# Sums of squares of k and q as two fp32r products, and the first modulation pieces in another shape, in a two-block transformer kernel

## What is computed

```
c_act = silu(c)
mod = c_act @ ada_w[layer] + ada_b[layer]                  # c is 1024 wide, ada_w[layer] 1024 x 6144
sh_m, sc_m, g_m, sh_f, sc_f, g_f = split(mod, 6)
h = rms_norm(x, pre_mix_g) * (1 + sc_m) + sh_m             # the input of the first product
...
k = rms_norm(k, k_norm_g)                                  # over the 64 elements of each head
q = rms_norm(q, q_norm_g)                                  # likewise
```

## Time and profile before

| | |
|---|---|
| median of 3 executions | 2051.48 us |
| the profiled execution | 2050.17 us, of which its span is 2048.5 us |
| TensorE matmuls busy | 1962.9 us, 96% of the span |
| TensorE weight loads busy | 1680.9 us, 82% |
| GpSimd busy | 999.8 us, 49% |
| VectorE busy | 793.4 us, 39% |
| ScalarE busy | 721.9 us, 35% |
| start of the first fp32r product | 52.92 us |
| stages k, v, q | about 768 to 913 us |

### The profile page before, as it was taken

The page is one execution under the profiler, slowest core; times in us unless marked ns, Lnnn a source line. Parts: engine busy times, 40 slices in busy tenths (PEclk is TensorE's granted clock), DMA queues, the critical chain, the costliest instruction groups (busy, mean ns, idle before and its releaser), DMA issues. The chain is left out here.

```text
span 2048.5 us, 28257 instructions
## 1 busy us (share of the span) xinstructions
PE 1962.9 (96%) x10884; PEld 1680.9 (82%) x10884; DVE 793.4 (39%) x1391; ACT 721.9 (35%) x1163; POOL 999.8 (49%) x541
## 2 busy tenths in 40 slices
PE   5999999999999989999998999999999999999998
PEld 5998887888888878877877888888876988767998
DVE  5666533444444045443634101110327760136212
ACT  2324325322221264344536222222524323345324
POOL 1634654466674434456643655554423443534652
PEclk9999999999999999999999999999999999999999
DMA  7655543465656313232112333333232334311132
GB/s 260 206 165 165 165 164 114 149 180 175 194 176 210 96 54 94 73 103 88 53 37 64 111 92 99 96 93 96 79 76 65 94 99 99 89 52 32 63 98 89
DMA packets 220325, 230.71 MB, mean 113 GB/s; under 512 B 15456, under 2 KB 185224, under 8 KB 219960
## 3 DMA queue, kind: packets, MB, share of 16 engines
q1 hardware_dynamic: 215392, 213.28, 34.6%
q10 hardware_dynamic: 4824, 15.88, 2.3%
HBM read 226.33 MB, written 2.79 MB: 112 GB/s over the span
## 5 line engine op out<-in xcount | busy, mean ns | idle before, releaser
L752 POOL TENSOR_TENSOR w_lo<-raw,w_hi 128x1024 fp32r<-128x1024 f32 (+1 forms) x296 | 731.1, 2484 | 575.6 <-ACT w_hi L745 575.6
L1424 PE MATMUL acc<-hh,w_hi 128*128 128x512 f32 (+1 forms) x1472 | 558.4, 379 | 17.3 <-DVE hl L2096 9.6
L1424 PE MATMUL acc<-hh,w_lo 128*128 128x512 f32 (+1 forms) x1472 | 549.4, 373 | 0.0
L1424 PE MATMUL acc<-hl,w_hi 128*128 128x512 f32 (+1 forms) x1472 | 549.3, 373 | 0.0
L745 ACT ACTIVATE w_hi<-raw 128x1024 fp32r<-128x1024 f32 (+1 forms) x296 | 308.2, 1051 | 394.9 <-DMA raw<-in_ffn_w_down 152.9
L1424 PEld LDWEIGHTS acc<-hh,w_hi 128*128 128x128 f32 x1472 | 280.7, 191 | 76.5 <-issue 18.6
L1424 PEld LDWEIGHTS acc<-hh,w_lo 128*128 128x128 f32 x1472 | 280.6, 191 | 48.6
L1424 PEld LDWEIGHTS acc<-hl,w_hi 128*128 128x128 f32 x1472 | 280.9, 191 | 47.8 <-issue 1.7
L1957 DVE SCALAR_TENSOR_TENSOR ada_wide<-ada_raw,c_act,ada_wide 128x1024 f32<-128x1024 f32 x84 | 167.2, 1991 | 85.2 <-DMA ada_raw<-in_ada_w 56.8
L1424 PE MATMUL acc<-w_hi,hh 128*128 128x256 f32 x672 | 194.0, 289 | 3.3 <-POOL hl L1305 3.3
L1424 PE MATMUL acc<-w_lo,hh 128*128 128x256 f32 x672 | 191.5, 285 | 0.0
(11 more groups left out here) (535 smaller groups left out, 2954.6 us busy)
## 6 DMA issues: line engine op xcount, KB each, us to landing
raw<-in_ffn_w_gu SPq DMA_DIRECT2D x176, 256.0 KB, 3.3
raw<-in_w_in SPq DMA_DIRECT2D x52, 512.0 KB, 3.6
ada_raw<-in_ada_w SPq DMA_DIRECT2D x50, 512.0 KB, 4.1
raw<-in_ffn_w_down SPq DMA_DIRECT2D x44, 512.0 KB, 3.7
raw<-in_a_w_in SPq DMA_DIRECT2D x32, 512.0 KB, 3.7
ada_raw<-in_ada_w ACTq DMA_DIRECT2D x30, 512.0 KB, 5.8
raw<-in_a_w_out SPq DMA_DIRECT2D x16, 512.0 KB, 3.7
ada_raw<-in_kv_ada_w SPq DMA_DIRECT2D x16, 512.0 KB, 5.0
```

What stands on the lines that cost most here:

```text
L752: eng.tensor_tensor(w_lo[:, s, part, :], raw[:, s, part, :], w_hi[:, s, part, :].bitcast(F32), ALU.subtract).then_inc(w_split, 1)
L1424: ins = pe.matmul(out, w, x, start=first and n == 0, stop=last and n == len(pairs) - 1, skip_group_check=check)
```

## The change

1. The squares of k and q are written twice by ScalarE, in fp32 (`sq`) and in fp32r (`sq_hi`); GpSimd subtracts them into `sq_lo` in the place of `sq`, in a new epilogue of its own (`low_squares`); TensorE sums them by two fp32r products with `head_ones_r`, and waits for GpSimd.
2. The first 2048 columns of `mod` are cut in eight other pieces of 1 MB: 512 columns by 512 rows of `ada_w`, in rows of 2 KB. Five go to VectorE, 4 instructions of 512 columns each. Three go to TensorE, now with `c_act` as the stationary operand (one column) and the weights moving, so that the result is a row of 512; ScalarE copies two such rows to SBUF and TensorE turns them into columns by products with a 1x1 one. The order of loads, sums and features around them is new, and the first square root's table is loaded ahead of `x`. The first two units of `mlp_v` are split by ScalarE between the copies of `x_first`.
3. The high parts of the first four chunks of `h2` are made ahead of the last copy of v.
4. Some semaphores are joined (`last_x` into `x_ready`, `last_sg` into `sg_ready`, `last_std` into `std_ready`), with no instruction moved.

The diff, cut to its core:

```diff
 # SP
-            next_step(0)
-            whole_step(ada_first[:, 0], 0, ada_first_in[0])
-            next_step(1)
+            dve_unit(0)
+            pe_unit(0)
+            dve_unit(1)
             sp.dma_start(x_tok[:], ...).then_inc(x_landed, 16)
-            for s in range(1, ADA_PE):
-                whole_step(ada_first[:, s], s, ada_first_in[s])
+            pe_unit(1)
             sp.wait_ge(x_landed, 16)
-            for s in range(2, ADA_SETUP - ADA_PE):
-                next_step(s)
-            load_group(sp, "mlp_v", 0, 0)
+            dve_unit(2)
+            pe_unit(2)
+            dve_unit(3)
+            load_unit(sp, S["mlp_v"], src_of["mlp_v"], 0, 0, 0)
+            dve_unit(4)
+            load_unit(sp, S["mlp_v"], src_of["mlp_v"], 0, 0, 1)
             load_group(sp, "mlp_v", 0, 1)
 # ScalarE
             act.wait_ge(c_ps, 1)
+            act.activation(head_ones_r[:], head_ones[:], ACT.Copy)
             act.activation(c_act[:], aux[:, 0, 0:DC], ACT.Silu).then_inc(c_ok, 1)
...
+            act.activation(warm[:], eps[:], ACT.Sqrt)
             act.wait_ge(x_landed, 16)
...
+            for wide, src in enumerate((ada_ps, bank(1))):
+                act.wait_ge(row_ps, wide + 1)
+                act.activation(ada_first[0:1, wide, 0, :], src[0:1, :], ACT.Copy).then_inc(row_sb, 1)
             for k in range(DC):
                 act.wait_ge(xt_ps, k + 1)
                 act.activation(x_first[:, k, :], XT_BANKS[k % len(XT_BANKS)], ACT.Copy).then_inc(kept_ready, 1)
-            split_hi(act, S["mlp_v"], 0, 0)
+                if k < 2:
+                    split_hi(act, S["mlp_v"], 0, 0, slice(k, k + 1))
...
                     for m in range(2):
-                        act.activation(sq[:, m, :], sums(j)[:, m, :], ACT.Square).then_inc(hsq_ready, 1)
+                        act.activation(sq[:, m, :], sums(j)[:, m, :], ACT.Square)
+                        act.activation(sq_hi[:, m, :], sums(j)[:, m, :], ACT.Square).then_inc(hsq_ready, 1)
...
                 if (i, j) == (1, 1):
                     log_sigmoid(gl_f[:, 1, :], 1)
+                    hi_chunks("h2", KU, hh, free=lambda k: S["q"].unit0 - 1 + RING)
                 tokens_epilogue(v_fox)(st, i, j)
...
-            hi_chunks("h2", DC, hh, free=lambda k: S["q"].unit0 - (k < KU) + RING)
+            hi_chunks("h2", DC - KU, hh, KU, free=lambda k: S["q"].unit0 + RING)
 # GpSimd
-            lead(pool, "k", split_lo, nothing, "v", unroll=True, started=True)
+            def low_squares(c0):
+                def epi(st, i, j):
+                    for m in range(2):
+                        pool.wait_ge(hsq_ready, c0 + 4 * i + 2 * j + m + 1)
+                        pool.tensor_tensor(sq_lo[:, m, :], sq[:, m, :], sq_hi[:, m, :].bitcast(F32), ALU.subtract).then_inc(hsq_split, 1)
+                return epi
+            lead(pool, "k", split_lo, low_squares(0), "v", unroll=True, started=True)
...
-            lead(pool, "q", split_lo, nothing, "gate", unroll=True)
+            lead(pool, "q", split_lo, low_squares(8), "gate", unroll=True)
 # TensorE
-                        pe.matmul(bank(0)[:, 2 * s + m:2 * s + m + 1], ada_first[:, s, k, m * P:(m + 1) * P], c_act[:, k:k + 1],
-                                  start=k == 0, stop=k == DC - 1)
+                    ins = pe.matmul(dst, c_act[:, KU * half + k:KU * half + k + 1], ada_unit_home(s)[:, k, :],
+                                    start=half == 0 and k == 0, stop=half == 1 and k == KU - 1)
...
-                    pe.wait_ge(hsq_ready, t + 1)
+                    pe.wait_ge(hsq_split, t + 1)
                     if t >= 2:
                         pe.wait_ge(hstd, t - 1)
-                    pe.matmul(aux[:, t % 2, :], head_ones[:], sq[:, t % 2, :], start=True, stop=True).then_inc(hs_ps, 1)
+                    products(aux[:, t % 2, :], ((head_ones_r[:], sq_hi[:, t % 2, :]), (head_ones_r[:], sq_lo[:, t % 2, :])), True, True).then_inc(hs_ps, 1)
 # VectorE
+            ada_unit(0)
+            ada_unit(1)
+            for n, (dst, r) in enumerate(((par_a, 112), (par_b, 104), (par_c, 74))):
+                dve.wait_ge(par_t, n + 1)
+                dve.tensor_copy(dst[:, 0:r], bank(1 + n)[:, 0:r]).then_inc(par_ok, 1)
+            inverse_deviation(0)
...
+            ada_unit(2)
+            ada_unit(3)
+            ada_unit(4)
             dve.wait_ge(ada_first_ps, 1)
```

More of the change, by code:

```diff
@@ L156, in build_program @@
         head_ones = place("head_ones", [P, P])
+        head_ones_r = place("head_ones_r", [P, P], F32R)
         par_a = place("par_a", [P, 112])
@@ L1607, in wide_beside, with row_columns, setup_sums @@
                 return before_chunk
-            def column_sums(dst, src):
-                for m in range(2):
-                    ins = pe.matmul(dst[:, m:m + 1], src[:, m * P:(m + 1) * P], ones[:, 0:1], start=True, stop=True)
+            def row_columns(wide):
+                pe.wait_ge(row_sb, wide + 1)
+                for m in range(4):
+                    pe.matmul(bank(0)[:, 4 * wide + m:4 * wide + m + 1], ada_first[0:1, wide, 0, m * P:(m + 1) * P], ones[0:1, 0:1],
+                              start=True, stop=True)
+            def setup_sums(wide, at):
+                pe.wait_ge(ada_setup_ready, at)
+                for m in range(4):
+                    ins = pe.matmul(bank(0)[:, 4 * wide + m:4 * wide + m + 1], ada_setup[:, wide - 1, m * P:(m + 1) * P], ones[:, 0:1],
+                                    start=True, stop=True)
                 return ins
@@ L1646, in _ @@
                 pe.transpose(bank(1 + n)[:, 0:r], rows[0:r, n, :], ident[0:r, 0:r]).then_inc(par_t, 1)
+            setup_sums(2, 1)
+            row_unit(1, ada_ps[0:1, :]).then_inc(row_ps, 1)
             pe.wait_ge(par_ok, 3)
+            row_unit(2, bank(1)[0:1, :])
+            pe.wait_ge(ada_setup_ready, 2)
+            pe.matmul(bank(1)[0:1, :], ones[:, 0:1], ada_setup[:, 0, :], start=False, stop=True).then_inc(row_ps, 1)
+            row_columns(0)
             first_to_features()
[L1649 to L1654 removed]
             WS_BANKS = [aux[:, 0, :], aux[:, 1, :], ms[:], ada_ps[:]]
@@ L1966, in wide_finish, with ada_unit @@
             def wide_finish(q):
-                dve.wait_ge(ada_sum, ADA_SETUP - ADA_PAIRS + q + 1)
+                dve.wait_ge(ada_sum, q + 1)
                 cols = slice(2 * ADA_SETUP + DC * q, 2 * ADA_SETUP + DC * (q + 1))
                 dve.tensor_tensor(mod[:, cols], ada_ps[:, 0:DC], par_a[:, cols], ALU.add).then_inc(ada_col, 1)
[L1972 to L1975, removed]
-                    else:
-                        if kk:
-                            dve.drain()
-                        ins = dve.scalar_tensor_tensor(total, w[:, kk, :], c_act[:, k0 + kk:k0 + kk + 1], total, ALU.mult, ALU.add)
-                return ins
-            def ada_finish(step, par, summed):
-                dve.wait_ge(ada_sum, summed)
-                dve.tensor_tensor(mod[:, ds(2 * step, 2)], ada_ps[:, 2 * par:2 * par + 2], par_a[:, ds(2 * step, 2)], ALU.add) \
-                    .then_inc(ada_col, 1)
+            def ada_unit(n):
+                wide, half = ADA_DVE[n]
+                total = ada_setup[:, wide - 1, :]
+                dve.wait_ge(ada_next_in[n], 16)
+                for kk in range(KU):
+                    k = KU * half + kk
+                    if kk == 0 and (half == 0 or wide == 1):
+                        dve.tensor_scalar(total, ada_next[:, 1 + n, kk, :], c_act[:, k:k + 1], None, ALU.mult)
+                    else:
+                        dve.scalar_tensor_tensor(total, ada_next[:, 1 + n, kk, :], c_act[:, k:k + 1], total, ALU.mult, ALU.add)
+                    ins = dve.drain()
+                if half:
+                    ins.then_inc(ada_setup_ready, 1)
             def inverse_deviation(n):
```

98 lines of the change are left out of this document (47 added, 51 removed).

## The result

| | before | changed |
|---|---|---|
| median, us | 2050.54 (4 runs, 2048.11 to 2052.91) | 2035.78 (4 runs, 2033.00 to 2038.01) |
| ratio, 95% interval | | 0.9928 (0.9912 to 0.9944) |
| profiled execution, time / span, us | 2050.17 / 2048.5 | 2038.01 / 2036.3 |

The change takes 14.8 us off, with an interval of 11.5 to 18.0 us. The forecast was 2033.0, range 2028 to 2041: it is 2.8 us too low and inside its range. The profiled execution is the slowest of its four; its span is 12.2 us shorter than before.

The account below looks back on a forecast made before the run. The prediction took TensorE, hardly ever idle, as the bound. Setup 8.5, squares 6.4 and v to q 3.6 sum to 18.5 us, from 2050.17 to 2031.7; with the median 1.3 higher, 2033.0 us, range 2028 to 2041.

Parts of the forecast that it names:

- Squares: k and q: four fp32r matmuls replace two fp32 ones, 0.80 us saved for each of eight pairs, 6.4 us.
- the cover on GpSimd: k and q: the added square work stays hidden, with 3.7 us left before TensorE wants the next weights.
- rivals 2 to 4: k and q: late split or fp32 squares, 2039.4 each, together 0.09; GpSimd locked out by reciprocals, 2057, 0.03.
- From v to q: Start of q: earlier high parts of h2 remove TensorE's waits, 3.6 us less; 2 if GpSimd is late once.
- Setup: Start of the kernel: first product at 44.4 us instead of 52.92, 8.5 us less.
- The landing of VectorE's last piece: Setup: VectorE's last piece of weights lands at 33.0 us, or at 35.0 with 3.0 us a piece.
- GpSimd's splits fall onto this piece: Setup: two GpSimd splits at 34 to 39 us slow VectorE's last two instructions, ending at 39, not 36.3.
- the product 2.73 us later: Setup: the first product follows the start of normed at 40.6 us by 2.73 us, so at 43.3.
- The middle value of 44.4: Setup: first product's start, taken between 43.3 us and 45.4 us, the latter with 3.0 us a piece.
- rival 1: Setup: TensorE stays at half pace, first product at 48.7, setup gives 4.2 us, total 2037.3; chance 0.12.
- the sign of being wrong: Setup: first product starting past 48 us, with the features of x as what VectorE waits for.
- my doubt of it: Setup: old column products at half pace, though never idle, speak against sustained busy time raising the clock to 2.4 GHz.

Follow-up runs that it names:

- e4: Changed kernel without GpSimd's 16 subtractions, TensorE multiplying sq_hi twice: 2038.77 us, ratio 0.9934.
- e2: Kernel before the change with only the high parts of the first four h2 chunks made ahead of v's last copy: 2050.24 us, ratio 0.9993.
- e11: Held kernel without the early high parts for q, all eight made after v's last copy: 2038.45 us, ratio 0.9933.
- e6: Changed kernel with GpSimd's first two weight splits waiting for the end of VectorE's last piece: 2031.53 us, ratio 0.9905.
- e3: Changed kernel with the squares and the h2 part as before, so the setup alone is new: 2046.82 us, ratio 0.9977.
- e5: Changed kernel run again unaltered, as control: 2036.69 us, ratio 0.9932.
- e10: Changed kernel unaltered once more, as control of the third group: 2039.28 us, ratio 0.9931.
- held kernel: Changed kernel with GpSimd's first two weight splits waiting for VectorE's last piece, run twice: 2031.53 and 2033.26 us.
- e9: Second run of the held kernel, against the changed kernel on the same chip: 2033.26 us, ratio 0.9911.

## Why the prediction was right, and where it was not

**Squares: right.** 6.4 us forecast; alone 6.7 in the profile's stretch and 6.5 in the median. The step of 0.23 us and the cover on GpSimd held; e4 shows that the subtractions cost nothing, and no wait of TensorE for `w_lo` came in k and q (rivals 2 to 4 fall).

**From v to q: right.** 3.6 forecast; 3.9 in e2's stretch, 4.4 between e11 and e6. Squares and early parts together were put at 10.0 us and measure 10.4 in the profiles.

**Setup: one step wrong and one wait missed.** It was put at 8.5 us and gave 4.1 alone (e3). The landing of VectorE's last piece was put at 33.0 us and was 32.8. That GpSimd's splits fall onto this piece, ending it at 39, was right as a mechanism: it ended at 38.0 or 39.8, by how many of its four instructions the splits meet; one that is met lasts 2.7 us, not 2.4. That `normed` begins at 40.6 was near, too (40.3 or 41.6). The step that failed is "the product 2.73 us later". That distance came from the earlier trace rows, where all the features were long copied when `mod` came. Now TensorE has three chunks and ScalarE three copies behind `mod` (the prediction itself put only the fifth chunk ahead of it), and the distance is 4.3 us at full clock and 6.5 in the profiles with the wait for VectorE and the half clock behind it. What the product follows is the end of the features: by 2.64 us in both of these, by 2.93 in e6. The middle value of 44.4 met the first profile's 44.62 only because the collision was light in that execution and the lost distance made up for it: that was luck. In three other profiles with the same setup (e3, e5, e10) the start is 48.1, near rival 1's 48.7 and past the 48 us that the prediction named as the sign of being wrong. The mechanism behind that rival and that sign was not what happened: the features up to the fifth chunk ran at full pace, and VectorE hardly waited for it. It ended at 38.1 us in the first profile and 37.2 in e5, level with VectorE's piece or ahead of it, though 1 to 2 us later than the 36 forecast, which is why the held kernel gains no more at the first product. The half pace came later, behind the wait for VectorE. A slip in the sum is small beside this: by its own terms, pieces of 3.0 us land the last one at 34.7 us, not 35.0.

The row pieces began at half pace, 6.51 us for the second, and ended at full, 3.60 for the third, in one train without a gap, and were done at 30.3 us (near 31 forecast). That agrees with the Trainium skill (TensorE: Matmul & The Clock Gate, What's actually happening), by which sustained busy time raises the clock; my doubt of it, from the column products of the earlier trace rows, was not borne out for rows of 512.

What the sum also lacked: GpSimd's low parts of the second group's weights stand behind the eight of `h0`. In the first profile TensorE waits 1.47 us ahead of the second group, since the first now runs at full pace (11.8 us, before 13.3):

```profile
54.38 5.71 POOL L760 TENSOR_TENSOR w_lo<-raw,w_hi 128x1024 fp32r<-128x1024 f32 x2
...
57.84 0.36 PE L1452 MATMUL acc<-w_hi,hh 128*128 128x256 f32 x1 [1.47 <-DVE v L2202]
```

The row names VectorE's addition of v, but e5's second group starts at 61.31 us, before its addition has begun (61.35), so it is the first of the two low parts, which ends at 57.74. The second addition of v is 8.15 us earlier in the first profile, and 4.7 in e5.

**The sum.** 18.5 us forecast, 14.8 measured. In the profiles the setup (up to the second addition of v) gives 4.7 to 8.2 us and the stretch from k to the attention 10.4. By the first profile, 8.2 + 10.4 = 18.6 us came, and unchanged code gave back 6.4 to leave a span shorter by 12.2. By e5 it was 4.7 + 10.3 = 15.0 with 0.4 given back, by e10 15.1 with 8.1 given back. My range had room for these stretches, but the sum had no term for them.

A version that beats both kernels is the held one: the median of its ten runs is 2032.8 us, that of the changed kernel's eleven beside it 2037.8.

## What to carry to other kernels

Read a distance between two engines ("the product comes 2.7 us behind `normed`") only with the other things that were ready by then; once an early load moves them together, whatever stands behind the wait in each queue becomes part of it. Where two engines hinder each other on the critical path, one that has time to spare can be made to wait for the other with a single semaphore: here the held splits end 0.5 us later than in the changed kernel's first profile, and the first product still starts earlier. It took some 3 us off by the profiles and 5 to 6 by the medians. And with gains of a few us, compare the stretch that was touched in several profiles of the same kernel: from k to the attention it repeated to 0.3 us where the whole differed by 7.5, and in the setup the same comparison showed two cases 3.5 us apart that one profile would have hidden.

## What the runs showed of the hardware

A wait of TensorE can cost more than its own length. Features of 16 passes took 1.95 us without the wait and 3.58 us behind an idle time of 2.75, with a granted clock of 0.61 in that stretch, and so in all three profiles with this wait. It is not so after every such wait: behind the 2.64 us ahead of the first product the granted clock stays at 1.00 from 44 to 48 us in the changed kernel's first profile, behind 2.94 us in e9 too, and behind 2.92 us in e6 it is 0.57. Short stretches near half clock come also in trains without a gap (0.71 at 250 to 254 us), in some executions and not in others. I could not find what decides that, and no experiment here set it off at will.

VectorE's instruction of 512 columns took 0.75 us alone (at most 753 ns with GpSimd held) and up to 2.72 us beside GpSimd's subtractions. The tile view of `ada_next` (least, median and most ns of the four) in e5 and then in e6:

```profile
L2024 DVE SCALAR_TENSOR_TENSOR ada_setup<-ada_next,c_act,ada_setup x4: 752/1712/2724, 32.7 to 37.1; 128x512 f32<-128x512 f32 x4
```

```profile
L2025 DVE SCALAR_TENSOR_TENSOR ada_setup<-ada_next,c_act,ada_setup x4: 751/752/753, 32.8 to 35.2; 128x512 f32<-128x512 f32 x4
```

This agrees with the Trainium skill (SBUF — State Buffer, Who interferes with whom), which describes the port pair of these two engines as an exclusive lock. What a plan must add is the order in which the two start: a start of GpSimd at 34.16 or 34.47 us, ahead of or behind VectorE's third instruction, decides whether two instructions are caught or one, and so 2 us on VectorE and 3.5 us at the first product.
